# Splitting the last layer norm of a streaming encoder layer among VectorE, ScalarE and GpSimd, with its weight and bias kept in PSUM

## What is computed

```python
def layer_norm(x, g, b):
    xf = x.astype(jnp.float32)
    mu = xf.mean(-1, keepdims=True)
    var = jnp.square(xf - mu).mean(-1, keepdims=True)
    return ((xf - mu) * lax.rsqrt(var + LN_EPS)).astype(x.dtype) * g + b
...
    x = layer_norm(ALPHA * x + h, ln2_g, ln2_b)
    x = layer_norm(ALPHA * x + 0.5 * swiglu(x, ffn2_w_up, ffn2_w_down), ln3_g, ln3_b)
    return x, new_buf, S_new
```

## Time and profile before

| | us |
|---|---|
| median of 3 runs (lowest, highest) | 1852.17 (1848.53, 1855.16) |
| profiled execution, its own time | 1849.95 |
| span of the profiled execution, first to last instruction | 1848.2 |
| TensorE busy | 1810.4 |
| VectorE busy | 1259.5 |
| ScalarE busy | 617.7 |
| GpSimd busy | 566.2 |

### The profile page before, as it was taken

How to read it: one execution, slowest core, us unless ns; L and a number is a source line. 1 busy time by engine, 2 the same in 40 slices (tenths; PEclk the granted TensorE clock), 3 DMA queues, 4 the chain that set the end, 5 groups by cost and what they waited for, 6 DMA issues and landing times.

```text
span 1848.2 us, 27128 instructions
## 1 busy us (share of the span) xinstructions
PE 1810.4 (98%) x11020; PEld 1682.6 (91%) x11020; DVE 1259.5 (68%) x1646; ACT 617.7 (33%) x1043; POOL 566.2 (31%) x374
## 2 busy tenths in 40 slices
PE   9999999999999999999999999999999999999996
PEld 8889899898999999999898898988988989899894
DVE  7758486667787778633667565675857758486566
ACT  5325233242544444410421505214114325233240
POOL 3324232233332222124323233232333324232230
PEclk9999999999999999999999999999999999999998
DMA  7342423424543434258457485675963342423402
GB/s 265 126 136 70 137 77 129 134 72 149 166 143 109 124 105 134 66 204 283 158 189 271 159 289 193 201 258 170 376 218 113 126 137 69 137 78 128 134 27 102
DMA packets 89611, 284.72 MB, mean 154 GB/s; under 512 B 8848, under 2 KB 11280, under 8 KB 89232
## 3 DMA queue, kind: packets, MB, share of 16 engines
q1 hardware_dynamic: 41984, 154.42, 26.6%
q10 hardware_dynamic: 30224, 66.70, 9.9%
q0 software_dynamic: 17280, 61.87, 9.5%
HBM read 245.66 MB, written 37.30 MB: 153 GB/s over the span
## 4 chain that ended last, share of the span: by engine, by line
PE 90%; DVE 6%; issue 1%; DMA 1%; ACT 1%; POOL 0%; POOLq 0%; DVEq 0%; SPq 0%; ACTq 0%
PE ps L642 89%; DVE wql L1500 2%; DMA wh<-in_weights 1%; PE ps L984 1%; DVE z L1783 1%; DVE ct L1500 1%; DVE z L1786 1%; DVE z L1748 1%; DVE stats L1771 0%; DVE tl L1500 0%; DMA raw<-in_weights 0%; POOL wl L567 0%; DVE quad_s L1500 0%; PE ps L929 0%; ACT xh L1126 0%
## 5 line engine op out<-in xcount | busy, mean ns | idle before, releaser
L567 POOL TENSOR_TENSOR wl<-raw,wh 128x1024 fp32r<-128x1024 f32 x118 | 299.3, 2539 | 83.1 <-DMA wh<-in_weights 73.6
L642 PE MATMUL ps<-th,wql 128*128 128x320 f32 x1040 | 321.3, 309 | 0.5 <-ACT pu L1126 0.5
L642 PE MATMUL ps<-th,wqh 128*128 128x320 f32 x1040 | 321.1, 309 | 0.0
L642 PE MATMUL ps<-tl,wqh 128*128 128x320 f32 x1040 | 320.6, 308 | 0.0
L551 POOL DMA_DIRECT2D wh<-in_weights x116 | 65.4, 564 | 635.4 <-PE ps L642 582.5
L1126 ACT ACTIVATE pu<-ps 128x320 f32<-128x320 f32 x195 | 85.4, 438 | 517.6 <-PE ps L642 517.6
L1500 DVE TENSOR_TENSOR wql<-qraw,wqh 128x512 fp32r<-128x512 f32 x195 | 242.2, 1242 | 21.5 <-ACT wqh L1126 21.5
L642 PE MATMUL ps<-xh,wql 128*128 128x320 f32 x780 | 240.5, 308 | 1.8 <-DVE ct L1500 1.8
L642 PE MATMUL ps<-xl,wqh 128*128 128x320 f32 x780 | 240.5, 308 | 0.0
L642 PE MATMUL ps<-xh,wqh 128*128 128x320 f32 x780 | 240.5, 308 | 0.0
L1500 DVE TENSOR_TENSOR wql<-quad_s,wqh 128x512 fp32r<-128x512 f32 (+1 forms) x195 | 178.9, 917 | 54.0 <-ACT wqh L1126 53.6
(11 more groups left out here) (190 smaller groups left out, 3779.4 us busy)
## 6 DMA issues: line engine op xcount, KB each, us to landing
qraw<-in_quads SPq DMA_DIRECT2D x130, 512.0 KB, 3.6
raw<-in_weights SPq DMA_DIRECT2D x120, 512.0 KB, 3.8
wh<-in_weights POOLq DMA_DIRECT2D x116, 512.0 KB, 5.2
state<-in_state_ret ACTq DMA_DIRECT2D x48, 512.0 KB, 7.6
out_ret_sample<-state ACTq DMA_DIRECT2D x32, 512.0 KB, 6.0
qk_scratch<-ctp SPq DMA_DIRECT2D x8, 640.0 KB, 5.6
z<-gate_c_scratch SPq DMA_DIRECT2D x4, 640.0 KB, 6.2
mix_scratch<-z ACTq DMA_DIRECT2D x4, 640.0 KB, 7.6
```

Of the source, the lines that this page charges most:

```text
L567: pool.tensor_tensor(wl[:, r, part], raw[:, r, part], wh[:, r, part].bitcast(f32), ALU.subtract).then_inc(chunk_split, 1)
L642: ins = nc.tensor.matmul(out, lhs, rhs, start=start, stop=stop, skip_group_check=adds)
```

## The change

The general stage `end_stage` is no longer used for the last norm; `last_stage` takes its place.

- Weight and bias are copied by ScalarE from SBUF into four PSUM banks that the early sums have left (four copies of 128x512), once VectorE has freed them. Ahead of these copies ScalarE takes the root of one column (`root_ready`), so that the root's table is loaded there.
- VectorE makes the output of tile 0, of tile 4, and of the second half of tile 3, with the same two instructions as before, which now read weight and bias from PSUM (`finish`).
- Tiles 1 and 2 and the first half of tile 3 go over ScalarE and GpSimd: VectorE makes minus mean times inverse deviation for them (`scales`) and signals; ScalarE computes z * inverse deviation + that (`normalise`); GpSimd multiplies by the weight and adds the bias, reading `lng` and `lnb` in SBUF.
- The late sums and their statistics alternate, tile by tile, and all of them stand behind the output of tile 0.
- In the second chain the steps that combined two small tensors are replaced by `tensor_scalar` steps of one column each, with the other operand as a per-partition scalar (`by_column`). The step that adds epsilon and the one that computes -0.5 t + 1.5 keep their form, over two columns.
- The stores move from ScalarE's queue to SyncE's, and that of tile 3 is cut into two of 256 KB.

```diff
@@ sync @@
+            def store(ready, n, t, part=slice(0, D)):
+                sync.wait_ge(ready, n)
+                dst = a["y_prompt"][t * 128:(t + 1) * 128, part] if t < PT else a["y_sample"][:, part]
+                sync.dma_start(dst, z[:, t, part]).then_inc(y_out, 16)
+
+            store(last_ready, 1, 0)
+            store(last_scaled, 1, 1)
+            store(last_scaled, 2, 2)
+            store(last_ready, 2, TT - 1)
+            store(last_ready, 3, TT - 2, slice(D // 2, D))
+            store(last_scaled, 3, TT - 2, slice(0, D // 2))
@@ gpsimd @@
+            pool.wait_ge(ln_in, 32 * 3)
+            for n, (t, part) in enumerate(((1, slice(0, D)), (2, slice(0, D)), (TT - 2, slice(0, D // 2)))):
+                pool.wait_ge(scaled, n + 1)
+                pool.tensor_tensor(z[:, t, part], z[:, t, part], lng[:, part], ALU.mult).then_inc(last_step, 1)
+                pool.wait_ge(last_step, n + 1)
+                pool.tensor_tensor(z[:, t, part], z[:, t, part], lnb[:, part], ALU.add).then_inc(last_scaled, 1)
@@ scalar @@
+            def normalise(n, t, part=slice(0, D)):
+                act.wait_ge(scales_asked, n)
+                nc.scalar.activation(z[:, t, part], z[:, t, part], ACT.Identity, bias=rt[:, 0, t:t + 1],
+                                     scale=rt[:, 2, t:t + 1]).then_inc(scaled, 1)
+
+            d0 = bk.at - 2 * TT
+            nc.scalar.activation(root_ready[:, :], ones[:, 0:1].bitcast(f32), ACT.Sqrt)
+            act.wait_ge(ln_in, 32 * 3)
+            for n, v in enumerate((lng, lnb)):
+                act.wait_ge(psum_free, d0 + 2 * n + 4)
+                b = (d0 + 2 * n + 2) % 8
+                for half in range(2):
+                    copy(ps[:, b + half, :], cols(half, 512, v[:, :])).then_inc(norm_in_psum, 1)
             roots(0, EARLY)
+            normalise(1, 1)
+            normalise(1, 2)
             roots(EARLY, TT)
-            for t in range(TT):
-                act.wait_ge(z_ready, 2 * TT + t + 1)
-                dst = a["y_prompt"][t * 128:(t + 1) * 128, :] if t < PT else a["y_sample"]
-                act.dma_start(dst, z[:, t, :]).then_inc(y_out, 16)
-            act.wait_ge(y_out, 16 * TT)
+            normalise(2, TT - 2, slice(0, D // 2))
+            act.wait_ge(y_out, 16 * (TT + 1))
@@ vector, inv_root @@
-                step(tt(t, inv, inv, ALU.mult))
-                after()
-                step(tt(t, t, rt[:, 0, c0:c1], ALU.mult))
+                if by_column:
+                    for c in range(c0, c1):
+                        v = rt[:, 2, c:c + 1]
+                        step(V.tensor_scalar(rt[:, 3, c:c + 1], v, v, rt[:, 0, c:c + 1], ALU.mult, ALU.mult))
+                else:
+                    step(tt(t, inv, inv, ALU.mult))
+                    after()
+                    step(tt(t, t, rt[:, 0, c0:c1], ALU.mult))
                 after()
                 step(V.tensor_scalar(t, t, -0.5, 1.5, ALU.mult, ALU.add))
                 after()
-                step(tt(inv, inv, t, ALU.mult))
+                if by_column:
+                    for c in range(c0, c1):
+                        v = rt[:, 2, c:c + 1]
+                        step(V.tensor_scalar(v, v, rt[:, 3, c:c + 1], None, ALU.mult))
+                else:
+                    step(tt(inv, inv, t, ALU.mult))
                 after()
@@ vector, the last stage @@
-            end_stage(3, 0.5 / ALPHA, transpose=False)
+            def scales(tiles):
+                for t in tiles:
+                    step(V.tensor_scalar(rt[:, 0, t:t + 1], mv[:, t, 0:1], rt[:, 2, t:t + 1], -1.0,
+                                         ALU.mult, ALU.mult))
+                after()
+                V.memset(mv[:, TT, 0:1], 0.0).then_inc(scales_asked, 1)
+
+            def last_stage(scale):
+                early, late, d0 = range(EARLY), range(EARLY, TT), bk.at
+                weight, bias = (ps[:, (d0 + n) % 8:(d0 + n) % 8 + 2, :].rearrange("p a b -> p (a b)") for n in (2, 4))
+
+                def finish(t, part=slice(0, D)):
+                    step(V.scalar_tensor_tensor(out=z[:, t, part], in0=z[:, t, part], scalar=mv[:, t, 0:1],
+                                                in1=weight[:, part], op0=ALU.subtract, op1=ALU.mult))
+                    after()
+                    V.scalar_tensor_tensor(out=z[:, t, part], in0=z[:, t, part], scalar=rt[:, 2, t:t + 1],
+                                           in1=bias[:, part], op0=ALU.mult, op1=ALU.add).then_inc(last_ready, 1)
+
+                for half in range(2):
+                    for t in early:
+                        down(scale, half, [t])
+                        moments(half, [t])
+                inv_deviation(early)
+                scales((1, 2))
+                dve.wait_ge(norm_in_psum, 4)
+                finish(0)
+                for half in range(2):
+                    for t in late:
+                        down(scale, half, [t])
+                        moments(half, [t])
+                inv_deviation(late, by_column=True)
+                scales((TT - 2,))
+                finish(TT - 1)
+                finish(TT - 2, slice(D // 2, D))
+            last_stage(0.5 / ALPHA)
```

More of the change, by code:

```diff
@@ L223, in build_layer @@
         odd_even = sb("odd_even", [128, 2])
+        root_ready = sb("root_ready", [128, 1])
         cache = sb("cache", [128, KT, NS_, 2])
@@ L355, in build_layer @@
         z_ready = sem("z_ready")
+        last_ready, last_scaled, last_step = sem("last_ready"), sem("last_scaled"), sem("last_step")
+        scales_asked, scaled, norm_in_psum = sem("scales_asked"), sem("scaled"), sem("norm_in_psum")
         root_asked = sem("root_asked")
@@ L1750, in down, with inv_root @@
                 dve.wait_ge(psum_free, bk())
-            def inv_root(c0, c1, eps):
+            def inv_root(c0, c1, eps, by_column=False):
                 var, r, inv, t = mv[:, c0:c1, 1], rt[:, 1, c0:c1], rt[:, 2, c0:c1], rt[:, 3, c0:c1]
@@ L1771, in moments, with inv_deviation @@
                     step(V.bn_stats(stats[:, t, 6 * half:6 * half + 6], cols(half, 512, z[:, t, :])))
-            def inv_deviation(tiles):
+            def inv_deviation(tiles, by_column=False):
                 after()
@@ L1777, in inv_deviation @@
                 after()
-                inv_root(tiles[0], tiles[-1] + 1, LN_EPS / ALPHA ** 2)
+                inv_root(tiles[0], tiles[-1] + 1, LN_EPS / ALPHA ** 2, by_column)
             def scale_and_shift(tiles):
```

## The result

The changed kernel takes 1854.13 us (median of 20 runs, 1852.0 to 1858.49), the kernel before in the same sitting 1850.36 us (20 runs, 1848.25 to 1855.16). The ratio is 1.0019, 95% interval [1.0012, 1.0026]: some 3.5 us slower (3.8 by the two medians), where 4.0 us faster was forecast. That is within 0.3%, so "same" came true as a class, but the time lies 2.1 us above the upper end of the range, and with so many runs the sign is settled. The forecast started from 1852.17, the median of three runs; the 20 runs put the kernel before 1.8 us lower, so the gain forecast (4.0) says more than the time forecast (1848.2).

What follows compares the result with a forecast made beforehand. VectorE's work after 1825.50 was taken to bound the tail behind TensorE. Gain 4.0 us: 5.2 from work, less 1.5 for the lock, plus 0.3 from smaller stores; 1852.17 becomes 1848.2, range 1845.0 to 1852.0.

Steps and rivals of the forecast that it cites:

- the last of the sum: End of the kernel: the last 256 KB store lands 2.0 us after issue, at 1843.8; the span ends at 1844.2.
- 1840.8, earlier: GpSimd's half tile: its last instruction ends at 1840.8, before VectorE's end at 1841.38.
- GpSimd becomes the end: Rival, last stage: GpSimd's queue ends after 1845.6, at 3.6 us per instruction; about 1854 with 4.0 each; chance 0.04.
- the 0.05 for the unseen: Chance 0.05 left for something unseen, such as a shift of buffers by the new column; no size given.
- The change leaves TensorE's program alone, so only the tail can move: Whole kernel: only what follows the last matmul can change, a tail of 17.7 us in all.
- VectorE's end: Last stage: VectorE ends at 1839.88 undisturbed, at 1841.38 with the lock, against 1845.08 before.
- The lock: Second chain: GpSimd's second add holds the two-column L1804 until 1836.85, 1.50 us late; L1791 passes at under 0.1.
- missed by 0.1 us: Rival, second chain: L1791 finds the second add begun and is 2.4 us late; gain 3.1, 1849.1; chance 0.24.
- no lock: Rival, second chain: so small a step slips through at no cost; gain 5.5, 1846.7; chance 0.12.
- read for all sizes: Second chain: the skill's rule would stop the first one-column pair instead of L1804, adding about 0.3 us.

Runs made afterwards that it cites:

- e4: The changed kernel without the new column root_ready (the root that loads the table writes a spare column of rt): ratio 1.0009, median 1851.98 us.
- e7: e6 with every tensor_scalar of the second chain over one column at a time: ratio 0.9980, median 1847.10 us.
- e6: e4 with GpSimd taking tiles 1 and 2 alone and VectorE making both halves of tile 3: ratio 0.9987, median 1848.06 us.
- e13: e7 with an unused column of 16 floats, so that every later buffer moves by 64 bytes: ratio 0.9970, median 1845.52 us.
- e1: The kernel before, with GpSimd waiting at its end for VectorE's last tile and doing nothing: ratio 1.0027, median 1855.64 us.
- e3: The kernel before with the column root_ready added but unused, moving the buffers behind it by 32 bytes: ratio 1.0012, median 1852.43 us.
- e2: The kernel before, with GpSimd waiting for VectorE's last tile and then doing one operation over one column: ratio 1.0028, median 1855.52 us.
- e15: The kernel before with the operands of the 320-wide products moved by 32 bytes, hh and hl by 64: ratio 1.0003.
- e14: The kernel before with only hh, hl and what is placed at and behind them moved by 32 bytes: ratio 1.0002.

## Why the prediction was wrong

**The step that failed is the last of the sum, "so 2.0 after its issue: 1843.8, and the span ends at 1844.2".** It carried over from before that the span ends half a us behind the last landing. It took the end of the program to be the end of VectorE and its stores, and asked of GpSimd only when its last instruction ends ("1840.8, earlier"). The runs show in its place that the end is the latest of all engines' closings, and that GpSimd's costs 7.74 to 7.77 us after its last work or wait. With the forecast's own 1840.8 that would have given 1848.6, and an end at 1848.8: a loss of 0.6 instead of a gain of 4.0. e4 measured just this (1848.85). In the rival "GpSimd becomes the end" I priced it at 3.6 us per instruction; with the DRAIN counted, GpSimd was the end already at 2.4. The number could have been read: the closing instructions of the kernel before show a DRAIN of 10.2 us on GpSimd that nothing waited for.

**The shift of the buffers** was named, with no price, inside the 0.05 for the unseen. It is the rest of the miss: -4.0 was forecast; e4 stands at +1.4 (1851.98 less 1850.55); the changed kernel at +3.8 (1854.13 less 1850.36), so the shift adds 2.3, or 1.9 by the ratios.

**"The change leaves TensorE's program alone, so only the tail can move"** was thus half right. The program is the same, its pace isn't.

**Right, by e4, whose stage starts where that of before does:**
- VectorE's end: forecast 1841.38, measured 1841.26. In the changed kernel it is 1844.62, less the shift of 3.21 also 1841.41. So close a hit is partly luck. VectorE came to its second chain 0.6 earlier than forecast (aggregates at 1833.38 instead of 1833.96), which gained little, because the lock's end is set by GpSimd: L1804 (L1803 in e4) ended at 1836.56 instead of 1836.85, and behind it VectorE took 4.7 instead of 4.5.
- The lock. L1804 was to wait for the second add and end 1.50 late; it took 1.45 where it takes 0.17 undisturbed, so it ended 1.28 late. L1791 was to get in between two instructions of GpSimd, and did. It took 0.44, where 0.2 to 0.3 was said: 0.27 longer than undisturbed, where under 0.1 was forecast. The other two outcomes named for this gap (missed by 0.1 us; no lock) didn't come. e7 shows that it is the two columns: 0.21 for two single ones in the same place.
- The rule of the Trainium skill ("SBUF — State Buffer", section "Who interferes with whom"), read for all sizes, would have stopped the one-column steps too. They were not stopped: the pairs of 0.45, 0.46 and 0.21 ran inside instructions of GpSimd. Another page of the Trainium skill, "VectorE: DVE Perf Modes", section "Mode 2×_2P — use both read ports for one tensor", says that in this mode a tensor is split in half along its outermost non-unit dimension, one half for each port. The trace agrees for the forms it has: two columns can be split and were held, one can't and passed. Not explained by it is the two-column reciprocal, which passed as well (0.17 at 1837.78, inside the add); that page of the Trainium skill and these runs don't say whether it has the mode.
- Sums and statistics from PSUM (0.67 to 0.69) and the output reading weight and bias from PSUM (1.28) cost what they had cost, GpSimd running beside them. ScalarE wrote PSUM at 0.59 to 0.60 a copy. One table load of 1.28, at 1810.6.

**Off in size only:** the half output instructions of VectorE took 0.74 and 0.75 instead of 0.69; ScalarE's normalising 1.24 instead of 1.05, its half 0.81 instead of 0.62; a 256 KB store landed after 2.2 instead of 2.0. By the stores e4 gained 3.7 where 4.0 was forecast.

**What the change should have been.** GpSimd may be the helper only if it is done 7.8 us before the stores are. e6 satisfies that with two tiles instead of two and a half, and turns +1.4 into -2.7 (1848.06 less 1850.76). The one-column steps give 1.0 more by medians (e7) and 64 bytes of placement 1.9 more (e13): 5.5 us below before. The whole is clear of noise, the last two steps by themselves are not: their intervals overlap with those of the kernels that they start from. In e13 the DRAIN is again the last to end, but by 1 us only:

```profile
L199 POOLq DRAIN  x1: 10144/10144/10144, 1831.9 to 1831.9; - x1
...
L199 ACTq COMPARE_BRANCH  x1: 45/45/45, 1840.9 to 1840.9; - x1
```

What stays open: why 32 bytes change the pitch (only that they do, and for which operands, was shown), and what sets that of the down projection. The profiled head is 3.0 us longer at the last matmul, of which the pitch is 2.2. The remaining 0.8 has no cause that was found, and is not large: what the pitch leaves of this difference lies between -0.6 and +2.3 us over these traces, at 2.0 in e1, whose buffers stand where those of before do.

## What to carry to other kernels

The end of a program is the latest closing of any engine, so read the closing instructions of each before work is given to an idle one: an engine with slack in its work may have none in its DRAIN. In this kernel GpSimd needed 7.7 us behind its last work or wait.

A scratch buffer can cost time without being used, if large operands are placed behind it: one column of four bytes cost this kernel some 2 us. Put it at the end, or fill it up to 64 bytes, and measure the added buffer alone (e3) before the code that uses it.

Where VectorE's small `tensor_scalar` steps run beside GpSimd, write them one column at a time: two of them took 0.21 us where a single one over two columns took 1.45.

## What the hardware showed that was not expected

- GpSimd's closing DRAIN takes 7.74 us from an idle engine (e1) and 7.75 to 7.77 after its last instruction (before, changed, e2). ScalarE's took 0.01.
- The time between matmuls of 128x320 went from 146.43 to 146.67 ns with the operands in SBUF 32 bytes off a 64-byte grid, at a granted clock of 1.00 (e15 moves these operands off the grid and leaves `hh` and `hl` on it, e14 the other way round); that of the down projection ranged from 230.9 to 234.6 over all placements, and by 0.4 at one placement.
- A two-column `tensor_scalar` on VectorE was held by GpSimd's `tensor_tensor` to its end (1.45 us instead of 0.17); a one-column `tensor_scalar` (0.15 in e7), a two-column reciprocal (0.17), bank-wide sums from PSUM (0.67 to 0.69), `bn_stats` (0.69) and `bn_aggr` (0.28 for two) were not.
